# A two-layer decoder trunk on one core: a new order around the six layer norms, and the output with one buffer per tile

## The chip, the cores and the metric

The kernel runs on one core of a Trainium2 chip. Its time is the device time of one execution in microseconds (us). TensorE (PE) multiplies matrices, VectorE (DVE), ScalarE (ACT) and GpSimd (POOL) work on elements, and SyncE (SP) only issues transfers here. Each engine runs its own list of instructions in order and waits on semaphores that other engines raise.

## The reference, cut to what matters

512 prompt tokens and 8 new tokens, 1024 channels, all in float32, go through two layers. Each layer has three blocks, and each block ends in a layer norm of the residual:

```
for l in range(DEPTH):                       # DEPTH = 2
    y = LN(ALPHA * y + 0.5 * swiglu(y, ffn1_wi[l], ffn1_wo[l]))
    y = LN(ALPHA * y + mixer(y))             # layer 0 sparse attention, layer 1 pooling
    y = LN(ALPHA * y + 0.5 * swiglu(y, ffn2_wi[l], ffn2_wo[l]))
```

The last y is the output of 512 x 1024 and 8 x 1024 numbers. Keys, values and pooling states are outputs too.

## The kernel before, in words

The activations stay on the core, channels on the partitions: `xf` has 8 tiles d = 0..7 of 128 channels by 520 tokens. The tokens are worked in two halves h = 0, 1 of 260 columns, `cols(h)`. A float32 product is made of three passes in a faster format: `xh` and `xl` are the high and low parts of x, `w_hi` and `w_lo` those of the weights (`split_hi` on ACT, line 616, and `split_lo` on DVE, line 1672), and the products are w_hi·xh, w_lo·xh and w_hi·xl. POOL makes `xl` (line 2458). Weights come in chunks of 1 MB through SP's queue into two buffers.

The stages run in the order f0, pr, op, f1, f2, pl, f3: f0 to f3 are the four SwiGLU blocks, pr projects and attends, op is attention's output product, pl the pooling mixer. Six of them (f0, op, f1, f2, pl, f3) end in a layer norm, the **tail**. In it each of the two halves goes through the same steps:

- DVE adds the last products to tiles 6 and 7 (`last_residual`, lines 2278, 2071, 2133),
- ACT squares these two tiles (lines 786 and 797),
- PE sums tiles and squares over the channels with a matrix of 1/1024 (`stats`, line 1120; in pl `tile_stats`, line 1610),
- ACT squares the mean (`moments`, line 632), DVE makes 1/variance (`variance`, lines 1687 to 1691), ACT takes the root (`root`, line 636),
- DVE subtracts the mean from each tile and multiplies it by the root (`normalise`, lines 1698 and 1704), ACT applies gain and offset, once for `xh` (line 643) and once for `xf` (line 645) (`affine`; only `xf` after f2 and f3), POOL makes `xl`.

The products of half 0 of a stage's last group end before those of half 1, so the statistics of half 0 are made while PE still multiplies. The statistics of half 1 are handed to the next stage as a function (`left`, or `middle`), which PE calls in its `first_half`: the first two weight chunks j = 0, 1 of the next stage times half 0 of the new x, line 1071. Then it takes half 1 (line 1050). `first_half` serves pr, f1, f2 and f3, whose x comes from a tail, and f0, whose x comes from the input. `two_chunks` calls it.

`first_hi` on ACT (line 860) makes high parts of the third chunk of the next SwiGLU block; the tails of op, f1 and pl hold it (`follow`). The tail of f2 holds `state_columns` (`between`), ACT's copies of the pooling state.

Before it starts, `first_half` waits until both residuals of both halves are done (`s_free`) and until `w_lo` of its first chunk is there (`s_lo`).

At the end of the kernel PE transposes `xf` to token rows (line 1652), 10 pieces of 512 columns (5 token tiles i by 2 column halves q), ACT copies them out of PSUM (line 1015) into `y_out`, which has two buffers, and ACT issues one transfer per token tile (lines 1021 and 1023). Each transfer waits until the one before it has landed: `if i >= 1: act.wait_ge(s_out, 16 * i)`.

## Time and profile before

| | |
|---|---|
| time, median of 3 runs | 1952.11 us (1952.04 to 1952.92) |
| the profiled execution | 1952.89 us, span of its instructions 1950.6 us |
| PE busy | 1849.0 us (95%) |
| DVE busy | 1250.4 us (64%) |
| ACT busy | 875.7 us (45%) |
| POOL busy | 454.1 us (23%) |
| mean granted TensorE clock | 0.979 of full speed |

The span runs from the first to the last instruction; 2.3 us of the time lie around it. A row of the timeline gives the start in us from the span's start, the duration, engine, line, operation, output<-input and count; brackets hold the idle time of the engine before it and what ended it. Rows of consecutive like instructions are merged.

### The profile page before, as it was taken

To read this page: it belongs to the slowest core of one execution; us is meant where nothing else is said; L and a number is where in the kernel's file an instruction comes from. 1 tells how busy PE (TensorE), PEld (TensorE's weight loads), DVE (VectorE), ACT (ScalarE), POOL (GpSimd) and SP (SyncE) were. 2 spreads that over 40 slices of the span, in tenths; PEclk is the share of its full clock that TensorE was granted. 3 is DMA by queue.
4 is the path that set the end of the run, shared out by engine and by line. 5 is a ranking of instruction groups with operands and counts; after the bars stand their busy time and mean duration, and the time that the engine had idled before them with its cause. 6 is when DMAs were issued, how large, how long until landed. Compare 5 with 4: busy or idle time off the path is not lost.

```text
span 1950.6 us, 36339 instructions
## 1 busy us (share of the span) xinstructions
PE 1849.0 (95%) x14532; PEld 1768.8 (91%) x14532; DVE 1250.4 (64%) x1871; ACT 875.7 (45%) x1377; POOL 454.1 (23%) x339
## 2 busy tenths in 40 slices
PE   7999999999989899999999999999998699999996
PEld 7999999996976578999999999999997599999995
DVE  5888832446967525988852288888325798886223
ACT  4455542343334435655552265555413375556123
POOL 3000081241321446100054130000712430003520
PEclk9999999999989999999999999999999799999998
DMA  5333345271110133233332323333323023333221
GB/s 165 91 108 108 108 145 206 72 184 44 28 42 1 39 114 87 66 108 108 108 103 76 103 66 103 104 99 104 98 94 110 2 66 108 108 108 103 83 76 44
DMA packets 260086, 179.79 MB, mean 92 GB/s; under 512 B 10847, under 2 KB 256999, under 8 KB 259462
## 3 DMA queue, kind: packets, MB, share of 16 engines
q1 hardware_dynamic: 249952, 154.90, 27.3%
q0 software_dynamic: 2288, 13.54, 2.0%
q10 hardware_dynamic: 7742, 9.88, 1.9%
q8 instruction: 77, 1.26, 0.3%
q14 instruction: 27, 0.22, 0.0%
HBM read 169.62 MB, written 8.08 MB: 91 GB/s over the span
## 4 chain that ended last, share of the span: by engine, by line
PE 81%; DVE 9%; ACT 4%; issue 3%; DMA 1%; POOL 0%; SPq 0%; ACTq 0%; DVEq 0%; POOLq 0%
PE ps L1145 36%; PE ps L1050 29%; PE ps L1232 3%; PE ps L1423 2%; PE ps L1071 2%; PE ps L1437 2%; PE ps L1237 1%; PE ps L1120 1%; ACT w_hi L616 1%; PE ps L1325 1%; ACT xh L643 1%; ACT xf L645 1%; PE ps L1216 1%; PE ps L1311 1%; DVE w_lo L2172 1%
## 5 line engine op out<-in xcount | busy, mean ns | idle before, releaser
L1672 DVE TENSOR_TENSOR w_lo<-w_raw,w_hi 128x2048 fp32r<-128x2048 f32 (+1 forms) x70 | 173.1, 2473 | 288.1 <-ACT w_hi L616 288.1
L2335 POOL TENSOR_TENSOR hl<-hid_all,hh 128x520 fp32r<-128x520 f32 x88 | 139.6, 1623 | 838.3 <-ACT hh L910 838.3
L1050 PE MATMUL ps<-hh,w_hi 128*128 128x260 f32 x1408 | 293.5, 283 | 0.0
L1050 PE MATMUL ps<-hh,w_lo 128*128 128x260 f32 x1408 | 292.1, 282 | 0.0
L616 ACT CAST w_hi<-w_raw 128x2048 fp32r<-128x2048 f32 (+1 forms) x70 | 126.3, 1805 | 263.2 <-PE ps L1050 236.3
L1050 PEld LDWEIGHTS ps<-hh,w_lo 128*128 128x128 f32 x1408 | 224.4, 188 | 0.1
L1050 PEld LDWEIGHTS ps<-hh,w_hi 128*128 128x128 f32 x1408 | 224.2, 188 | 0.1
L870 ACT CAST w_hi<-w_sum 128x1024 fp32r<-128x1024 f32 x160 | 168.0, 1050 | 117.4 <-DVE w_sum L2154 104.5
L2172 DVE TENSOR_TENSOR w_lo<-w_sum,w_hi 128x1024 fp32r<-128x1024 f32 x160 | 194.8, 1217 | 4.5 <-ACT w_hi L870 4.5
L1050 PE MATMUL ps<-hl,w_hi 128*128 128x260 f32 x1408 | 178.0, 283 | 0.0
L1050 PEld LDWEIGHTS ps<-hl,w_hi 128*128 128x128 f32 x1408 | 172.8, 188 | 0.0
L1145 PE MATMUL ps<-xh,w_hi 128*128 128x260 f32 x640 | 160.4, 283 | 10.7 <-DVE silu_g L2188 6.6
L1145 PE MATMUL ps<-t_hi,w_hi 128*128 128x260 f32 x640 | 161.5, 284 | 0.6 <-DVE w_lo L2172 0.2
L1145 PE MATMUL ps<-t_hi,w_lo 128*128 128x260 f32 x640 | 160.6, 283 | 0.0
L1145 PE MATMUL ps<-xh,w_lo 128*128 128x260 f32 x640 | 159.4, 283 | 0.0
L1145 PEld LDWEIGHTS ps<-xh,w_hi 128*128 128x128 f32 x640 | 120.7, 189 | 13.2 <-DVE silu_g L2188 8.2
L884 ACT ACTIVATE hid_all<-ps 128x260 f32 (+1 forms) x160 | 60.5, 378 | 155.8 <-PE ps L1145 155.8
L1145 PEld LDWEIGHTS ps<-t_hi,w_hi 128*128 128x128 f32 x640 | 121.1, 189 | 1.8 <-issue 0.9
L1145 PEld LDWEIGHTS ps<-t_hi,w_lo 128*128 128x128 f32 x640 | 120.5, 188 | 0.0
L1145 PEld LDWEIGHTS ps<-xh,w_lo 128*128 128x128 f32 x640 | 120.3, 188 | 0.0
L2188 DVE TENSOR_TENSOR silu_g<-silu_g,ps 128x260 f32<-128x260 f32 x160 | 67.3, 420 | 65.6 <-PE ps L1145 62.5
L1145 PE MATMUL ps<-xl,w_hi 128*128 128x260 f32 x640 | 102.9, 283 | 0.0
(330 smaller groups left out, 4432.9 us busy)
## 6 DMA issues: line engine op xcount, KB each, us to landing
w_raw<-in_ffn_wi_dram SPq DMA_DIRECT2D x176, 512.0 KB
w_raw<-in_ffn_wo_dram SPq DMA_DIRECT2D x32, 1024.0 KB
w_raw<-in_ffn_wo_dram SPq DMA_DIRECT2D x16, 768.0 KB
w_raw<-in_attn_w_in_dram SPq DMA_DIRECT2D x8, 1024.0 KB
keys_scratch<-key_half POOLq DMA_DIRECT2D x2, 2048.0 KB, 9.9
w_raw<-in_attn_w_o_dram SPq DMA_DIRECT2D x4, 1024.0 KB
x_in<-in_x_prompt_dram ACTq DMA_DIRECT2D x4, 512.0 KB, 9.7
out_dram<-y_out ACTq DMA_DIRECT2D x4, 512.0 KB
```

The lines of the kernel that those rows point to most:

```text
L616: nc.scalar.copy(w_hi[:, c % 2, 0:n], w_raw[:, c % 2, 0:n]).then_inc(s_hi, 1)
L870: nc.scalar.copy(blocks(st, j)[1][0][:, x], w_sum[:, c % 2, x]).then_inc(s_sums_hi, 1)
L884: nc.scalar.activation(x[..., cols(h)], bank_of(j, b), ACT.Copy).then_inc(s_copy, 1)
L1050: mm = nc.tensor.matmul(ps[0:mc, bank + 2 * m + h, 0:HT], w[:, k, m, 0:mc], x(k)[:, h * HT:(h + 1) * HT], start=first and k == 0 and w is ...
L1071: nc.tensor.matmul(ps[:, 4 * j + 2 * m, 0:HT], w[j][:, k, m, :], x[:, k, cols(0)], start=start, stop=stop)
L1145: mm = nc.tensor.matmul(bank_of(j, bank[p]), w[:, k * P:(k + 1) * P], x[:, k, :], start=p in (1, 2, 4, 5) and k == 0 and w is wh and x is ...
L1232: nc.tensor.matmul(ps[0:mc, bank + h, 0:HT], w[:, k, m, 0:mc], xh[:, k, cols(h)], start=k == 0 and w is wh, stop=False)
L1423: mm = nc.tensor.matmul(ps[:, 2 + t % 2, r * P:(r + 1) * P], attn(B, r)[:, j * P:(j + 1) * P], diag[:, B % 2, r, :], start=True, stop=True)
L1672: nc.vector.tensor_tensor(w_lo[:, c % 2, 0:n], w_raw[:, c % 2, 0:n], w_hi[:, c % 2, 0:n].bitcast(F32), ALU.subtract).then_inc(s_lo, 1)
L2172: nc.vector.tensor_tensor(lo[:, x], w_sum[:, (st.chunk + j) % 2, x], hi[:, x].bitcast(F32), ALU.subtract).then_inc(s_sums_lo, 1)
L2188: nc.vector.tensor_tensor(x, x, bank_of(j, 0), ALU.add).then_inc(s_gate1 if h else s_gate0, 1)
L2335: nc.gpsimd.tensor_tensor(hl[:, k, :], hid_all[:, k, :], hh[:, k, :].bitcast(F32), ALU.subtract).then_inc(s_hl, 1)
```

## The change

Five things are done.

1. `tail` on ACT: after the statistics of half 0 the root comes first, then `split_hi(nxt)` where there is one, then `affine` for the first three tiles (`AHEAD`; none in f2), then `split_hi(nxt + 1)`, then the squares of half 1. Before, `split_hi(nxt + 1)` stood ahead of all `affine` steps, and two tiles (none in f2) ahead of the squares.
2. After the squares of half 1 come two tiles of `affine` instead of three, then `moments` of half 1, then the other tiles, and only then `first_hi` (before: ahead of `moments`).
3. `tail` on DVE: the first three tiles of half 0 are normalised directly after its variance, ahead of `split_lo(nxt)` and of the residual of half 1. Before, all eight came after that residual.
4. `first_half` on PE: chunk 0 takes three tiles, high and low parts, then the statistics of half 1 are made, then chunk 1 takes the three tiles, then both chunks go on tile by tile. The products are the same.
5. The output: `y_out` has five buffers; the ten pieces have an order and PSUM banks of their own, six are copied by ACT and four by DVE, SP issues the five transfers with no wait between them, and the first two pieces are copied by ACT in the tail of f3, ahead of the root of half 1.

```diff
-        y_out = at("y_out", [P, 2, D], offset=h_off)
+        y_out = at("y_out", [P, NQT + 1, D], offset=h_off)
...
+        Y_ORDER = ((0, 0), (0, 1), (1, 0), (1, 1), (2, 0), (3, 0), (4, 0), (2, 1), (3, 1), (4, 1))
+        Y_BANK = {(0, 0): 0, (0, 1): 1, (1, 0): 2, (1, 1): 3, (2, 0): 4, (3, 0): 6, (4, 0): 0, (2, 1): 1, (3, 1): 5, (4, 1): 7}
+        Y_ACT = ((0, 0), (0, 1), (2, 0), (3, 0), (4, 0), (4, 1))
+        Y_DVE = ((1, 0), (1, 1), (2, 1), (3, 1))
...
+        AHEAD = 3
...
@@ block.sync, at its end
+            for i in range(NQT + 1):
+                for of, s_y in ((Y_ACT, s_y_act), (Y_DVE, s_y_dve)):
+                    last = max((n + 1 for n, (t, _) in enumerate(of) if t == i), default=0)
+                    if last > 0:
+                        sp.wait_ge(s_y, last)
+                if i < NQT:
+                    sp.dma_start(outs[0][0, i * P:(i + 1) * P, :], y_out[:, i, :]).then_inc(s_out, 16)
+                else:
+                    sp.dma_start(outs[1].rearrange("b t d -> (b t) d"), y_out[0:DEC, i, :]).then_inc(s_out, 16)
+            sp.wait_ge(s_out, 16 * (NQT + 1))
@@ block.scalar, tail
                 moments(st, 0)
+                root(st, 0)
                 if nxt is not None and not early:
                     split_hi(nxt)
-                root(st, 0)
+                ahead = AHEAD if between is not state_columns else 0
+                affine(n, st, 0, split, order, 0, ahead)
                 if nxt is not None:
                     split_hi(nxt + 1)
-                ahead = 2 if between is None else 0
-                affine(n, st, 0, split, order, 0, ahead)
                 for d in range(KD - 2, KD):
                     act.wait_ge(s_free, first_free + d + 1)
                     nc.scalar.activation(sq[:, d % 2, cols(1)], xf[:, d, cols(1)], ACT.Square).then_inc(s_sq, 1)
-                affine(n, st, 0, split, order, ahead, ahead + 3)
+                affine(n, st, 0, split, order, ahead, ahead + 2)
+                moments(st, 1)
+                affine(n, st, 0, split, order, ahead + 2, KD)
                 if follow is not None:
                     first_hi(plan[follow], nth[follow], 2)
-                moments(st, 1)
-                affine(n, st, 0, split, order, ahead + 3, KD)
                 if between is not None:
                     between()
                 root(st, 1)
...
+            def output(n):
+                act.wait_ge(s_tr, KD + 1 + Y_ORDER.index(Y_ACT[n]) + 1)
+                dst, src = y_half(*Y_ACT[n])
+                nc.scalar.activation(dst, src, ACT.Copy).then_inc(s_y_act, 1)
+
+            def first_output():
+
+                for n in range(2):
+                    output(n)
...
-                     POOL_ORDER if before_pool else range(KD), state_columns if before_pool else None,
+                     POOL_ORDER if before_pool else range(KD), state_columns if before_pool else first_output if nxt is None else None,
...
-            for i in range(NQT + 1):
-                rows = P if i < NQT else DEC
-                for q in range(2):
-                    act.wait_ge(s_tr, KD + 1 + 2 * i + q + 1)
-                    nc.scalar.activation(y_out[0:rows, i % 2, q * 512:(q + 1) * 512], ps[0:rows, 2 * (i % 2) + q, :],
-                                         ACT.Copy).then_inc(s_ev, 1)
-                act.wait_ge(s_ev, KD + 2 * i + 2)
-                if i >= 1:
-                    act.wait_ge(s_out, 16 * i)
...
+            for n in range(2, len(Y_ACT)):
+                output(n)
@@ block.tensor, first_half
-                for k in range(KD + 2):
-                    if k < KD:
-                        pe.wait_ge(s_xh, first_x(st, 0) + k + 1)
-                        tile(0, wh, xh, k, k == 0, False)
-                        tile(0, wl, xh, k, False, False)
-                        if k == 0:
-                            pe.wait_ge(s_hi, st.chunk + 2)
-                        tile(1, wh, xh, k, k == 0, False)
-                    if k == 2 and middle is not None:
-                        middle()
-                    if k >= 2:
-                        pe.wait_ge(s_x, first_x(st, 0) + k - 1)
-                        tile(0, wh, xl, k - 2, False, k == KD + 1)
-                        tile(1, wh, xl, k - 2, False, False)
+
+                def high(j, k):
+                    pe.wait_ge(s_xh, first_x(st, 0) + k + 1)
+                    tile(j, wh, xh, k, k == 0, False)
+                    if j == 0:
+                        tile(0, wl, xh, k, False, False)
+
+                def low(j, k):
+                    pe.wait_ge(s_x, first_x(st, 0) + k + 1)
+                    tile(j, wh, xl, k, False, j == 0 and k == KD - 1)
+
+                for k in range(AHEAD):
+                    high(0, k)
+                for k in range(AHEAD):
+                    low(0, k)
+                if middle is not None:
+                    middle()
+                pe.wait_ge(s_hi, st.chunk + 2)
+                for k in range(AHEAD):
+                    high(1, k)
+                    low(1, k)
+                for k in range(AHEAD, KD):
+                    for j in range(2):
+                        high(j, k)
+                    if k > AHEAD:
+                        for j in range(2):
+                            low(j, k - 1)
+                for j in range(2):
+                    low(j, KD - 1)
@@ block.tensor, at its end
+            for i, q in Y_ORDER:
+                pe.wait_ge(s_xf, tot["t"] - (KD if i < 2 else KD // 2 if q == 0 else 0))
+                if (i, q) in ((4, 0), (2, 1)):
+                    pe.wait_ge(s_y_act, 2)
+                rows = y_rows(i)
+                for d in range(4):
+                    mm = nc.tensor.transpose(ps[0:rows, Y_BANK[i, q], d * P:(d + 1) * P], xf[:, 4 * q + d, i * P:i * P + rows], ident)
+                mm.then_inc(s_tr, 1)
@@ block.vector, tail
                 variance(st, eps, 0)
+                normalise(st, 0, order, 0, AHEAD)
                 if nxt is not None and not early:
                     split_lo(nxt)
                 last_residual(1)
-                normalise(st, 0, order)
+                normalise(st, 0, order, AHEAD, KD)
...
@@ block.vector, at its end
+            for i, q in Y_DVE:
+                dve.wait_ge(s_tr, KD + 1 + Y_ORDER.index((i, q)) + 1)
+                dst, src = y_half(i, q)
+                nc.vector.tensor_copy(dst, src).then_inc(s_y_dve, 1)
```

## Rows read from the trace of the kernel before

**Rows 1.** The page: the chain that ended last, by engine.

```profile
PE 81%; DVE 9%; ACT 4%; issue 3%; DMA 1%; POOL 0%; SPq 0%; ACTq 0%; DVEq 0%; POOLq 0%
```

**Rows 2.** Waits of PE: line, awaited, us in total, times, longest us.

```profile
PE ps L1071 <- ACT xh L643: 14.0, 4, 6.0
```

**Rows 3.** Timeline of PE in the tail of f0 and after.

```profile
384.03 0.48 PE L1071 MATMUL ps<-xh,w_hi 128*128 128x260 f32 x2 [2.64 <-ACT xh L643]
...
388.00 0.76 PE L1120 MATMUL ps<-sum_z,const 128*128 128x260 f32 x2
...
398.24 2.09 PE L1071 MATMUL ps<-xh,w_lo 128*128 128x260 f32 x16
```

**Rows 4.** Stretches there: us, busy (x count) of PE, PEld, DVE, ACT, POOL, clock, DMA share, GB/s.

```profile
384.00:388.00 4.00, 3.97 (x18) 3.60 (x19) 4.00 (x12) 4.00 (x10) 2.23 (x3) 0.61 0.38 56
```

**Rows 5.** Timeline of ACT in the tail of f0.

```profile
381.48 1.90 ACT L616 CAST w_hi<-w_raw 128x2048 fp32r<-128x2048 f32 x1 [2.12 <-PE ps L1050]
383.28 0.60 ACT L643 ACTIVATE xh<-xf,lnp 128x260 fp32r<-128x260 f32 x1
...
391.00 0.39 ACT L632 ACTIVATE hid<-ps 128x260 f32<-128x260 f32 x1 [2.04 <-PE ps L1120]
...
395.17 0.60 ACT L643 ACTIVATE xh<-xf,lnp 128x260 fp32r<-128x260 f32 x1 [0.54 <-DVE xf L1704]
...
399.64 0.59 ACT L645 ACTIVATE xf<-xf,lnp 128x260 f32<-128x260 f32 x1
```

**Rows 6.** Timeline of DVE in the tail of f0.

```profile
374.67 1.79 DVE L1691 RECIPROCAL ps<-ps 128x260 f32<-128x260 f32 x1
379.11 2.29 DVE L1672 TENSOR_TENSOR w_lo<-w_raw,w_hi 128x2048 fp32r<-128x2048 f32 x1 [2.65 <-ACT w_hi L616]
381.42 0.76 DVE L2278 SCALAR_TENSOR_TENSOR xf<-xf,ps 128x260 f32<-128x260 f32 x2
...
382.77 0.41 DVE L1704 TENSOR_TENSOR xf<-xf,ps 128x260 f32<-128x260 f32 x1
...
387.47 2.48 DVE L1672 TENSOR_TENSOR w_lo<-w_raw,w_hi 128x2048 fp32r<-128x2048 f32 x1
```

**Rows 7.** Timeline of POOL in the tail of f0, beside DVE's 387.47.

```profile
388.05 3.18 POOL L2458 TENSOR_TENSOR xl<-xf,xh 128x260 fp32r<-128x260 f32 x2 [0.25 <-ACT xf L645]
```

**Rows 8.** Stretches: PE with two short gaps after the last products (f3).

```profile
1921.50:1926.00 4.50, 3.02 (x14) 2.12 (x12) 4.30 (x13) 2.44 (x6) 0.00 (x0) 1.00 0.00 0
```

**Rows 9.** Timeline of ACT in the tail of op.

```profile
766.94 1.90 ACT L616 CAST w_hi<-w_raw 128x2048 fp32r<-128x2048 f32 x1 [0.33 <-PE ps L1050]
...
776.58 0.39 ACT L632 ACTIVATE hid<-ps 128x260 f32<-128x260 f32 x1 [0.79 <-PE ps L1120]
```

**Rows 10.** Timeline of ACT in the tail of pl.

```profile
1556.93 1.89 ACT L616 CAST w_hi<-w_raw 128x2048 fp32r<-128x2048 f32 x1
...
1564.30 1.47 ACT L860 CAST even_hi<-w_raw 128x1536 fp32r<-128x1536 f32 x1
...
1568.92 0.37 ACT L636 ACTIVATE ps<-ps 128x260 f32<-128x260 f32 x1
```

**Rows 11.** Timeline of DVE, the first step of f2 that awaits the whole tail of f1.

```profile
1154.31 1.56 DVE L2210 TENSOR_TENSOR t_sum<-xf 128x1040 f32<-128x1040 f32 x1 [1.56 <-ACT xf L645]
```

**Rows 12.** Timeline of ACT, the root of half 1 in the tail of f2.

```profile
1509.10 0.37 ACT L636 ACTIVATE ps<-ps 128x260 f32<-128x260 f32 x1 [1.74 <-DVE ps L1691]
```

**Rows 13.** Timeline of PE at the start, `first_half` of f0.

```profile
22.61 1.23 PE L1071 MATMUL ps<-xh,w_hi 128*128 128x260 f32 x4 [1.04 <-ACT w_hi L616]
```

**Rows 14.** Timeline of the tail of f3 and the output, all engines.

```profile
1928.68 3.67 PE L1652 MATMUL ps<-const,xf 128*128 128x128 f32 x16 [2.40 <-ACT xf L645]
...
1936.51 1.06 ACT L1015 ACTIVATE y_out<-ps 128x512 f32<-128x512 f32 x2
1937.60 0.36 ACTq L1021 DMA_DIRECT2D out_dram<-y_out  x1
...
1948.42 0.30 ACTq L1023 DMA_DIRECT2D out_dram<-y_out  x1
```

More of the change, by code:

```diff
@@ L358, in trunk_kernel @@
         s_out = sem("s_out")
+        s_y_act = sem("s_y_act")
+        s_y_dve = sem("s_y_dve")
         s_rope_in = sem("s_rope_in")
@@ L486, in trunk_kernel, with y_rows, y_half @@
         SQUARES = 10
+        Y_ORDER = ((0, 0), (0, 1), (1, 0), (1, 1), (2, 0), (3, 0), (4, 0), (2, 1), (3, 1), (4, 1))
+        Y_BANK = {(0, 0): 0, (0, 1): 1, (1, 0): 2, (1, 1): 3, (2, 0): 4, (3, 0): 6, (4, 0): 0, (2, 1): 1, (3, 1): 5, (4, 1): 7}
+        Y_ACT = ((0, 0), (0, 1), (2, 0), (3, 0), (4, 0), (4, 1))
+        Y_DVE = ((1, 0), (1, 1), (2, 1), (3, 1))
+        def y_rows(i):
+            return P if i < NQT else DEC
+        def y_half(i, q):
+            return y_out[0:y_rows(i), i, q * 512:(q + 1) * 512], ps[0:y_rows(i), Y_BANK[i, q], :]
+        AHEAD = 3
         SIDES = UNITS_OF + 4
@@ L1009, in _ @@
                     ffn(name, after[name])
-            for i in range(NQT + 1):
-                rows = P if i < NQT else DEC
-                for q in range(2):
-                    act.wait_ge(s_tr, KD + 1 + 2 * i + q + 1)
-                    nc.scalar.activation(y_out[0:rows, i % 2, q * 512:(q + 1) * 512], ps[0:rows, 2 * (i % 2) + q, :],
-                                         ACT.Copy).then_inc(s_ev, 1)
-                act.wait_ge(s_ev, KD + 2 * i + 2)
-                if i >= 1:
-                    act.wait_ge(s_out, 16 * i)
-                if i < NQT:
-                    act.dma_start(outs[0][0, i * P:(i + 1) * P, :], y_out[:, i % 2, :]).then_inc(s_out, 16)
-                else:
-                    act.dma_start(outs[1].rearrange("b t d -> (b t) d"), y_out[0:DEC, i % 2, :]).then_inc(s_out, 16)
-            act.wait_ge(s_out, 16 * (NQT + 1))
+            for n in range(2, len(Y_ACT)):
+                output(n)
             act.wait_ge(s_kvo, 16 * 6)
@@ L1644, in _ @@
             left()
-            for i in range(NQT + 1):
-                pe.wait_ge(s_xf, tot["t"] - (KD if i < 2 else 0))
-                rows = P if i < NQT else DEC
-                for q in range(2):
-                    if i >= 2:
-                        pe.wait_ge(s_ev, KD + 2 * (i - 2) + q + 1)
-                    for d in range(4):
-                        mm = nc.tensor.transpose(ps[0:rows, 2 * (i % 2) + q, d * P:(d + 1) * P],
-                                                 xf[:, 4 * q + d, i * P:i * P + rows], ident)
-                    mm.then_inc(s_tr, 1)
+            for i, q in Y_ORDER:
[6 more added lines that the diff above has]
+                mm.then_inc(s_tr, 1)
         @block.vector
@@ L1691, in variance, with normalise @@
                 nc.vector.reciprocal(v, v).then_inc(s_rv, 1)
-            def normalise(st, h, order):
-                n = []
-                for at_ in range(KD + 1):
-                    if at_ < KD:
+            def normalise(st, h, order, begin, end):
+                n = {}
+                for at_ in range(begin, end + 1):
+                    if at_ < end:
                         x = xf[:, order[at_], cols(h)]
-                        n.append(step(nc.vector.tensor_tensor(x, x, moment(0, h), ALU.subtract)))
-                    if at_ == 1:
+                        n[at_] = step(nc.vector.tensor_tensor(x, x, moment(0, h), ALU.subtract))
+                    if at_ == begin + 1:
                         dve.wait_ge(s_rstd, 2 * st.ln + h + 1)
-                    if at_ >= 1:
+                    if at_ > begin:
                         done(n[at_ - 1])
@@ L1717, in tail @@
                 variance(st, eps, 1)
-                normalise(st, 1, order)
+                normalise(st, 1, order, 0, KD)
             def rope_sin(li, m, bank):
```

## The prediction

> **What bounds the kernel now.** I read the page first. The chain that ended last is four fifths PE [rows 1], so only time in which PE idles or runs slowly before the last tail, and the stretch after PE's last product, can be won. Next the waits of PE: the dearest is `first_half` waiting for the first `xh` of a normalised x, four times, 14.0 us [rows 2]. The timeline around one of them shows the pattern: PE ends f0's products at 381.4, idles 2.64 us, restarts at 384.03 [rows 3], and for the next 4 us its granted clock is 0.61 of full, the level of 1.2 GHz for most of it [rows 4]. The products of `first_half` start 0.12 us apart at full clock (16 in 2.09 with the last one's drain) and 0.22 apart at half. In PE's own terms the tail of f0 holds 96 products (11.5 us) and the statistics of half 1 (2.6 us), 14.1 us, and takes from 381.4 to 400.2, 18.8: 4.6 lost, 2.6 to the idle gap and 2.0 to the clock. Then I laid ACT and DVE beside it [rows 5, 6]: both have nothing to do before the products end and are full after. Last the end of the kernel [rows 14]: the five transfers of the output are issued from 1937.60 to 1948.42, every 2.70 us, one after the landing of the other.
>
> **The change part by part.** Times are of the profiled execution; steps are start to start. One subtract or multiply of DVE is 0.336 us (14 of them from 382.77 to 387.47), so a tile is 0.67 [rows 6]. One `affine` instruction is 0.50 (9 steps from 395.17 to 399.64), so a tile with `xh` and `xf` is 0.99 [rows 5].
>
> *Tail of f0 into pr.* DVE's 1/variance ends at 376.46; three tiles (2.0 us) and the root (0.37) then fit before `split_lo` at 379.11, in an idle stretch of 2.65 [rows 6]. ACT splits the next chunk until 379.0 as before, and applies three tiles until 381.96 (2.97), while PE still multiplies. The second split can only start when the last product frees its buffer, at 381.48 [rows 5], so it comes 0.5 late. POOL's first `xl` now fall on `split_lo`. Beside one, POOL needed 3.18 for two and DVE 2.48 instead of 2.29 [rows 6, 7]: I add 0.2 to the residual (bounds 0 and 0.2). PE waits for that residual, 381.6 + 0.7, and starts at 382.5 instead of 384.03. The gap is 1.1 us. In the tail of f3 PE has gaps of 0.61 and 0.87 in 4.5 us and the clock stays 1.00 [rows 8], so I take full clock here. 18 products of chunk 0 (2.2), statistics done 2.96 after their start (the distance from 388.00 to the mean's square at 391.00 [rows 3, 5]) at 387.65, `first_half` ends at 382.5 + 14.1 = 396.6 instead of 400.2: 3.5 won. Does x come in time? On ACT: split, squares and two tiles until 386.4, mean's square at 387.65, three tiles until 390.9, root, first tile of half 1 at 391.8, instead of 395.17 [rows 5]. Its eighth `xh` is there at 399.4; PE needs it at 396.6 + 7 x 0.48 = 400.0. It holds by 0.6. **3.5**, bounds 2.5 and 3.7.
>
> *Tail of f1 into f2.* The same, but `first_hi` (1.37 a step) now stands between the last tile of half 0 and the root, and delays it: half 1 starts on ACT 2.0 us earlier, not 3.4. Its eighth `xh` is now late for PE by about a microsecond, and DVE's `t_sum`, which follows ACT's last `xf` at once [rows 11] and heads an unbroken chain of DVE to PE's fifth product of the stage, moves by the same 2.0. **2.0**, bounds 1.2 and 2.8.
>
> *Tail of op into f1.* Its products of half 1 are short, so 1/variance ends at 766.2, 0.7 before they end. The three tiles (2.0) now push the residual from 766.89 to 768.2, so PE starts only 0.4 earlier (769.05 for 769.49), and ACT starts its first tile at 767.3 where it started the split at 766.94 [rows 9]. From there ACT is full: the list split, tiles, squares, mean, `first_hi`, root took 11.99 us in pl with no gap (1556.93 to 1568.92) [rows 10], and the new order has the same entries. So 0.36 is lost at the front and the 0.79 before the mean's square [rows 9] is won, if the statistics are in time. 0.4, less a bit for the clock, which with a gap of 2.2 us may fall here. **0.3**, bounds -0.5 and 0.9.
>
> *Tail of pl into f3.* Here ACT had no gap at all [rows 10]. It now waits for the first normalised tile (1557.6 instead of 1556.93) and the root of half 1 comes 0.65 later. PE's gap of 6 us stays, because the residual of half 1 is now behind three tiles. **-0.6**, bounds -1.2 and 0.
>
> *Tail of f2 into pl.* DVE bounds this stage. Three tiles leave its list, 2.0, and the root finds ACT idle 1.74 before [rows 12]. **1.7**, bounds 1.2 and 2.0.
>
> *Start of f0.* PE waits 1.04 for the second split [rows 13]; 18 products of chunk 0 now fill it, at 0.22 each. Four or five of them, worth 0.12 later. **0.6**, bounds 0 and 1.04.
>
> *Tail of f3 and output.* The last product ends at 1921.65. DVE normalises five tiles instead of eight after the residual, 1922.4 to 1925.8 (was 1927.7), 1/variance is ready at 1928.4 (was 1930.4). But ACT now awaits two transposed pieces. PE gets half 0 at 1927.1; four transposes take 0.92 (16 in 3.67 at half clock) and a copy 0.53 [rows 14], so the second copy ends and the root starts at 1929.5, 1.1 after it could. `xf` is complete at 1935.6, 1.0 earlier. Then the last three pieces are transposed until 1938.0 (0.92, 0.92, 0.5). ACT has four copies from 1935.6, the last at 1938.1; DVE four of about 0.6 (its copies are not in this stretch; I take ACT's price), the last at 1937.7. So SP issues tile 0 at about 1930, tile 1 at 1936.2, 2 at 1937.4, 3 at 1938.4, the short one at 1938.8. The last issue before was at 1948.42 and the span ended 2.2 later. With 2.2 to 2.7 to land, and 0.3 for transfers in each other's way, the span ends at 1941.3 instead of 1950.6. **9.3**, bounds 8 and 10.5 (the clock of the last transposes is worth 1).
>
> The Trainium skill (DMA: Bandwidth & Descriptors, Anatomy of one DMA) puts a transfer at about 2.0 us fixed and the bytes at 436 GB/s, as an estimate 3.2 us for 512 KB; the trace shows an issue every 2.70. By the page the end would be some 0.5 later.
>
> Sum: 3.5 + 2.0 + 0.3 - 0.6 + 1.7 + 0.6 + 9.3 = 16.8. The profiled execution took 1952.89 (span 1950.6 and 2.3 around it), so 1936.1; the median of the runs lies 0.8 below it, so **1935.3 us**.
>
> **The rivals.**
>
> *A, the clock falls all the same* in the tails of f0 and f1. For it: it stood at 1.00 until after PE had restarted at 384.03, so it does not answer to the gap at once [rows 3, 4]. Against: the gap is 1.1, not 2.64, and [rows 8]. 3.1 us at half (4.00 at 0.61 [rows 4]) would cost 1.6 in each: gain 13.6, 1938.5. Beside it, the Trainium skill (TensorE: Matmul & The Clock Gate, A second HAM failure mode) says that frequent short idle spells can make the clock swing between its levels; the stretch with two such spells does not show it.
>
> *B, the transfers do not overlap*: each of the last three takes its 2.7 behind the other. From 1936.2 that is 1944.3, and 2.2 for the short one: 1946.5, 5.2 less, 1940.5. For it: all are on the same 16 engines. Against: most of the 2.7 need not be data; nothing shown here tells.
>
> *C, the tails give nothing*: ACT's list is as long as before, and in op and pl it sets the pace. If it does in f0 and f1 too, only the output gains: 1942.8. Against: ACT idles 2.12 before the split at 381.48 and 2.04 before the mean's square [rows 5].
>
> *D, slower*: PE's new order begins every `first_half` with a burst and then waits for the residual, POOL or the statistics, and the clock stays at half through it. Each product at half costs 0.10 to 0.12 more; `first_half` has 96, five times. From 172 products more at half (21 us) the kernel is slower by over 0.2%; all of four tails would cost 46 less 17, 1981. Against: the rows show full clock again from about 388.2 under steady products [rows 4].
>
> **How the numbers follow.** Forecast 0.66, A 0.13, B 0.10, C 0.08, D 0.03. The time is that of the forecast. Its bounds, all at the good end, give 1931.2; all at the bad end 1941. The range of 1931.0 to 1940.5 holds the forecast nearly whole, A and half of B. About 0.2% (3.9 us) is what a measurement of this kernel can tell from no change. Forecast, A, B and C are faster by more: 0.95 with a little off for several shortfalls together; same 0.02, slower 0.03.
>
> **What would show it.** In the changed profile: the wait of `first_half` for `xh` is down from 14.0 to about 6 (pl alone), with PE's gap after f0 and f1 near 1.1 and the clock 1.00 in the 4 us behind it; on ACT in f1 `first_hi` directly ahead of the root; the residual in op and pl behind three tiles; the root in f3 about 1 us after DVE's reciprocal, behind two copies; five issues on SP, the last some 17 us after PE's last product of f3 (it was 26.8). The prediction is wrong if the clock is at half in f0 and f1, if the last landing comes more than 21 us after PE's last product, or if a wait for POOL's `xl` appears in `first_half`.

## The result and the profile after

The changed kernel takes 1936.07 us (median of 4 runs, 1933.81 to 1936.65) beside 1952.07 (1949.44 to 1952.92) of the kernel before on the same chip: ratio 0.9913, 95% interval 0.9901 to 0.9925. That is 16.0 us less. The forecast was 1935.3, the range 1931.0 to 1940.5. The profiled execution took 1936.2, its span 1933.9.

To say where the time came from, I cut both spans at instructions that both kernels have: DVE's last residuals, DVE's `t_sum`, PE's w_lo·xh products of chunk 1 of `first_half` (merged as x16). The columns are differences of start times in the two profiles; the last row runs from the step of DVE that f3's last product releases to the end of the span. "None" marks a stretch for which the prediction had no term.

| stretch | before | after | gain | predicted |
|---|---|---|---|---|
| span start to f0's first product with `t_hi` | 49.86 | 48.83 | 1.0 | 0.6 |
| f0's residual of half 1 to the x16 products of pr | 16.82 | 13.17 | 3.65 | 3.5 |
| from there through attention to op's residual of half 0 | 359.40 | 359.78 | -0.4 | none |
| from there to the `t_sum` of f1 | 31.20 | 30.54 | 0.66 | 0.3 |
| f1's residual of half 0 to the `t_sum` of f2 | 34.34 | 32.16 | 2.18 | 2.0 |
| f2's residual of half 1 to pl's residual of half 0 | 48.73 | 46.74 | 2.0 | 1.7 |
| pl's 1/variance of half 0 to the `t_sum` of f3 | 23.09 | 24.57 | -1.5 | -0.6 |
| f3's last product to the end | 28.9 | 19.9 | 9.0 | 9.3 |

They sum to 16.7, the difference of the spans; predicted were 16.8. (The products between these stretches take the same time to 0.05 us.)

Timeline of PE in the changed kernel, in the tail of f0, where [rows 3] are those of before:

```profile
381.26 0.47 PE L1093 MATMUL ps<-xh,w_hi 128*128 128x260 f32 x2 [0.90 <-DVE w_lo L1707]
...
383.49 0.60 PE L1157 MATMUL ps<-sum_z,const 128*128 128x260 f32 x2
...
393.57 2.09 PE L1093 MATMUL ps<-xh,w_lo 128*128 128x260 f32 x16
```

PE idles 0.90 us instead of 2.64. Stretches of 4 us that begin at the restarts in f0 and op and around the one in f1 (columns as in [rows 4], which showed 0.61):

```profile
381.20:385.20 4.00, 3.94 (x26) 3.77 (x27) 4.00 (x11) 4.00 (x7) 1.86 (x3) 1.00 0.78 139
764.60:768.60 4.00, 3.84 (x25) 3.48 (x26) 4.00 (x11) 4.00 (x7) 1.76 (x3) 1.00 0.00 0
1128.00:1132.00 4.00, 3.48 (x24) 3.37 (x25) 4.00 (x13) 4.00 (x7) 1.85 (x4) 1.00 0.80 231
```

The clock is at its upper level in all three. ACT in the same tail [rows 5] has no idle time before the split, and 0.87 instead of 2.04 before the mean's square:

```profile
380.94 1.90 ACT L640 CAST w_hi<-w_raw 128x2048 fp32r<-128x2048 f32 x1
...
386.32 0.39 ACT L656 ACTIVATE hid<-ps 128x260 f32<-128x260 f32 x1 [0.87 <-PE ps L1157]
...
390.50 0.61 ACT L667 ACTIVATE xh<-xf,lnp 128x260 fp32r<-128x260 f32 x1 [0.55 <-DVE xf L1739]
```

The waits of PE in `first_half` (columns as in [rows 2], where ACT's `xh` stood with 14.0): what is left is one gap in pl, one in op and two short ones in f0 and f1.

```profile
PE ps L1093 <- DVE xf L2169: 6.1, 1, 6.1
PE ps L1093 <- DVE xf L2107: 2.1, 1, 2.1
PE ps L1093 <- DVE w_lo L1707: 1.8, 2, 0.9
```

Timeline of ACT in the tail of pl: the mean's square of half 1 before, with no idle time ahead of it (the rest in [rows 10]), and then the changed kernel:

```profile
1565.67 0.38 ACT L632 ACTIVATE hid<-ps 128x260 f32<-128x260 f32 x1
```

```profile
1548.46 0.60 ACT L667 ACTIVATE xh<-xf,lnp 128x260 fp32r<-128x260 f32 x1 [0.61 <-DVE xf L1739]
...
1556.64 0.39 ACT L656 ACTIVATE hid<-ps 128x260 f32<-128x260 f32 x1 [0.69 <-PE ps L1647]
...
1559.90 1.47 ACT L894 CAST even_hi<-w_raw 128x1536 fp32r<-128x1536 f32 x1
1561.27 0.38 ACT L660 ACTIVATE ps<-ps 128x260 f32<-128x260 f32 x1
```

This list had no gap before. Now it has two, 0.61 and 0.69, and `first_hi` (1.37 a step) stands directly ahead of root. One more thing differs there. PE restarts 4.6 and 4.7 us behind the start of 1/variance of half 0 in the two kernels, after a gap of 6.0 to 6.1 us and at half clock, but in the changed kernel the clock comes back later. The stretch of 3 us that begins 7.6 us behind 1/variance, before and after:

```profile
1562.40:1565.40 3.00, 3.00 (x20) 2.77 (x19) 2.99 (x2) 3.00 (x6) 2.65 (x2) 0.98 0.00 0
```

```profile
1553.30:1556.30 3.00, 3.00 (x15) 2.73 (x14) 2.48 (x2) 2.65 (x7) 1.26 (x1) 0.71 0.00 0
```

The statistics of half 1 end 10.95 us behind 1/variance instead of 10.17.

The end of the kernel, timeline of PE, DVE and ACT and then SP's issues ([rows 14] before):

```profile
1921.10 0.38 ACT L660 ACTIVATE ps<-ps 128x260 f32<-128x260 f32 x1
1924.65 5.38 PE L1688 MATMUL ps<-const,xf 128*128 128x128 f32 x24 [2.37 <-ACT xf L669]
1929.21 0.69 DVE L2347 COPY y_out<-ps 128x512 f32<-128x512 f32 x1 [0.16 <-PE ps L1688]
1930.07 0.59 ACT L874 ACTIVATE y_out<-ps 8x512 f32<-8x512 f32 x1 [1.54 <-PE ps L1688]
1921.23 0.37 SPq L628 DMA_DIRECT2D out_dram<-y_out  x1
1927.53 0.37 SPq L628 DMA_DIRECT2D out_dram<-y_out  x1
...
1930.68 0.31 SPq L630 DMA_DIRECT2D out_dram<-y_out  x1
```

The last product releases DVE at 1913.99; the last issue comes 16.7 behind that and the end 19.9 (before 26.8 and 28.9).

### The profile page after: what moved, and what is told of

The parts are those of the page before. It is cut to its first block, busy times and chain, and to the rows that moved or that the text cites. A ratio compares the mean times of both kernels' runs of the same rounds, so it can differ in the third digit from the quotient of the medians.

```text
span 1933.9 us, 36347 instructions
## 1 busy us (share of the span) xinstructions
PE 1849.3 (96%) x14532; PEld 1768.4 (91%) x14532; DVE 1251.2 (65%) x1875; ACT 874.0 (45%) x1373; POOL 453.0 (23%) x339
## 4 chain that ended last, share of the span: by engine, by line
PE 82%; DVE 8%; ACT 5%; issue 3%; DMA 1%; POOL 0%; ACTq 0%; DVEq 0%; POOLq 0%
PE ps L1182 36%; PE ps L1072 29%; PE ps L1269 3%; PE ps L1460 2%; PE ps L1474 2%; PE ps L1093 2%; PE ps L1274 1%; PE ps L1157 1%; PE ps L1362 1%; ACT xf L669 1%; ACT xh L667 1%; ACT w_hi L640 1%; PE ps L1253 1%; PE ps L1348 1%; DVE w_lo L2208 1%
```

## The experiments

Each run was timed against the kernel before on its own chip; a ratio stands with its interval. An execution's start and its attention part differ from run to run by up to 2.6 us each (below), so verdicts rest on the stretches of the table above, which in the runs that leave them alone repeat to 0.05 us for f0, op and f1, to 0.2 for f2, to 0.4 for the last one and to 0.8 for pl. The last two differ with the moment at which the clock comes back in them. In pl that moment is 8.9 to 9.4 us behind 1/variance where the stretch takes 24.35 to 24.58 (five executions), and 10.4 and 10.5 where it takes 25.06 and 25.14. In the last stretch it is 13.6 us behind the last product, amid the last transposes, where the stretch takes 19.6, and 16.5, behind all of them, where it takes 19.9. Pl and the last stretch are therefore to be compared between executions with like clocks.

**1. Output alone.** The changed kernel with ACT's and DVE's tail and `first_half` as before.

```diff
-                normalise(st, 0, order, 0, AHEAD)
...
-                for k in range(AHEAD):
-                    high(0, k)
...
+                for k in range(KD + 2):
```

> The new output alone (five buffers, SP's transfers, the order of the pieces, the first two copies in the tail of f3); tails and first_half as before. Terms add: in the tail of f3 the two copies delay the root of half 1 by 0.5, PE transposes the last 24 tiles in 5.4 us from the fourth xf tile of half 1 on, and the span ends 3.9 after it, near 1943.9, 6.7 shorter than 1950.6, with everything before f3's last product where it was (1921.7). Rival (the output gains only together with the shorter tail of f3): under 4 us. Ratio to the kernel before 0.9966 by the first, above 0.998 by the second.

1946.35 us (1945.61 to 1948.21), ratio 0.9967 (0.9955 to 0.998). From the last product to the end 22.2 instead of 28.9: 6.8. The tails are as before: 17.14, 31.30, 34.40, 48.75 and 23.09 in the order of the table, with the 2.64 gap behind f0.

**2. Tails alone.** The kernel before with the new tails and the new `first_half`, and its own output.

```diff
+        AHEAD = 3
...
-                for k in range(KD + 2):
+                for k in range(AHEAD):
+                    high(0, k)
```

> The new tails and first_half alone, output as before with two buffers and a transfer awaiting the one before. Terms add: f3's last product 7.7 us earlier as in the changed kernel, in f3 the normalisation of three tiles ahead gives 2.0 more, the transfers are then issued 2.70 apart as before: span 9.7 shorter, near 1940.9, ratio 0.995. Rival (the tails' gain is given back later, in attention or by slower transfers): less than 7.

1942.86 us (1941.54 to 1943.33), ratio 0.9948 (0.9932 to 0.9965). The stretches are those of the changed kernel (13.17, 30.53, 32.16, 46.72, 24.58), and the last one is 26.9, 2.0 less than before: DVE's part of the new tail gives that in f3. 6.8 and 2.0 are 8.8 of the 9.0, so the two halves add up and neither needs the other. No run tells PE's new order (part 4 of the change) from the new lists of ACT and DVE (parts 1 to 3).

**3. One transfer behind the other.** Tests rival B.

```diff
+                if i > 0:
+                    sp.wait_ge(s_out, 16 * i)
                 if i < NQT:
                     sp.dma_start(outs[0][0, i * P:(i + 1) * P, :], y_out[:, i, :]).then_inc(s_out, 16)
```

> The changed kernel, but each of SP's five transfers awaits the landing of the one before; five buffers, copies and transposes unchanged. If the overlap of the transfers carries the output's gain: tile 1 is issued at the same place (13.6 us after f3's last product), tiles 2 and 3 and the short one 2.7 apart behind it, and the end is 3.9 later than in the changed kernel (span 1937.8). Rival (the last three transfers are bound by the bytes that the queue moves, so waiting costs little): under 1 us later.

From the last product to the end 23.8 instead of 19.9, and SP's issues again every 2.70 us: the overlap is worth 3.8 (4.2 beside the executions with 19.6). The time is 1938.63 us (1937.08 to 1940.35), ratio 0.9931 (0.9915 to 0.9948). The profiled span, 1934.8, is only 0.9 longer than the changed kernel's, because its start was 0.9 and its attention part 2.6 shorter. The windows of the changed kernel between 1930 and 1932 show what overlapped transfers share: 406 GB/s, so 1.29 us for 512 KB. The rest of the 2.70 is no data: in the kernel before, where transfers also went one by one, 1.2 us of each step move nothing.

```profile
1939.80:1941.00 1.20, 1.08 (x6) 0.68 (x4) 0.00 (x0) 0.28 (x1) 0.00 (x0) 0.50 0.00 0
```

**4. PE held.** Tests what gap and clock are worth by giving both back: PE starts `first_half` of pr and f2 only at the fourth `xh`.

```diff
+                if st in (plan["pr"], plan["f2"]):
+                    pe.wait_ge(s_xh, first_x(st, 0) + AHEAD + 1)
```

> The changed kernel, but in pr and f2 PE's first_half waits for the fourth xh tile of half 0 before it starts, which puts back a gap of about 3.6 us after the products of f0 and f1 (0.9 in the changed kernel). If a gap of this length costs the clock too, as in the kernel before: granted clock 0.5 for about 3 us behind the restart and 3.6 to 4.3 us lost in each of the two, 7 to 8 in all. Rival (the clock does not fall, the half clock of the kernel before had another cause): 2.7 us each, 5.4 in all, clock 1.00.

1945.11 us (1943.5 to 1947.97), ratio 0.9962 (0.9948 to 0.9976). The stretch of f0 takes 18.95 instead of 13.17, that of f1 36.72 instead of 32.16: 5.8 and 4.6, of which the longer gap (3.85 instead of 0.90) is 2.95 each. The rest, 2.8 and 1.6, fits the clock: in f0 it was at half until 6.1 us behind the restart, in f1 from 1.4 to 4.8 behind it. The end moved by 8.9, with the start and attention 1.4 shorter in this run. Timeline and stretch behind the restart in f0:

```profile
383.67 0.77 PE L1093 MATMUL ps<-xh,w_hi 128*128 128x260 f32 x2 [3.85 <-ACT xh L667]
```

```profile
384.00:388.00 4.00, 4.00 (x19) 4.00 (x19) 2.16 (x1) 0.90 (x2) 3.46 (x2) 0.50 0.13 19
```

19 products in 4 us where the changed kernel does 27. The rival, a gap at full clock, falls.

**5. Residual first** in op and pl (the two tails for which `early` is true), on DVE and, with the second split, on ACT. DVE's part:

```diff
                 variance(st, eps, 0)
+                if early:
+                    last_residual(1)
                 normalise(st, 0, order, 0, AHEAD)
```

> The changed kernel with one part set back in op and pl alone: VectorE adds the residual of half 1 ahead of the three normalised tiles instead of behind them, and ScalarE writes the xh of the next stage's second tile ahead of the normalised tiles instead of behind. Theory (the loss of 1.5 us in pl comes from starting the tiles before the residual, since ScalarE's tiles then wait for root and xh): from the residual to pl's last sum of half 1 0.8 to 1.5 us less than the 20.9 us of the changed kernel, and op 0 to 0.7 us more than its 20.1; in all about 0.8 us earlier than the changed kernel. Rival (the loss in pl comes from the place of first_hi behind the moments, which this run keeps): pl's stretch stays within 0.2 us, and the end with it.

1937.47 us (1936.55 to 1939.15), ratio 0.9922 (0.9909 to 0.9936). Both expectations miss. Pl takes 25.18; the clock came back late in it (10.5), and with that the unchanged pl takes 25.06 and 25.14. Op takes 32.64 instead of 30.54: 2.1 worse, more than before the change. PE's timeline and the stretch behind it in op:

```profile
763.36 0.48 PE L1095 MATMUL ps<-xh,w_hi 128*128 128x260 f32 x2 [2.64 <-ACT xh L667]
```

```profile
763.30:767.30 4.00, 3.75 (x17) 3.33 (x18) 4.00 (x12) 4.00 (x10) 2.23 (x3) 0.65 0.00 0
```

The gap is 2.64 again and the clock falls. PE also waits 0.18 for its second `xh`, and the statistics end 2.3 us later than in the changed kernel, where the gap was 2.12 and the clock stayed at 1.00. ACT has nothing ahead of them to do and waits 2.28.

**6. `first_hi` ahead of `moments`** in op, f1 and pl, as it was.

```diff
+                if follow is not None:
+                    first_hi(plan[follow], nth[follow], 2)
                 moments(st, 1)
                 affine(n, st, 0, split, order, ahead + 2, KD)
-                if follow is not None:
-                    first_hi(plan[follow], nth[follow], 2)
```

> The changed kernel with one part set back: the next half's first xh (first_hi) is issued on ScalarE ahead of the moments' sums and normalised tiles of half 1 instead of behind them, in op, f1 and pl. Theory: ScalarE stood idle 0.87 us in f1 and 0.69 us in pl ahead of the moments, and first_hi of 1.3 us stood straight ahead of root in f1 and pl, with 1.23 us of idle time on VectorE behind it; set back it fills the idle time, so f1's stretch from residual to last sum is 0.9 us shorter than 19.5, pl's 0.7 shorter than 20.9, op's the same: 1.6 us in all. Rival: the moments and the root are then late by the whole of first_hi less the idle time, 0.4 to 0.6 us later, and nothing or a small loss comes of it.

1934.21 us (1933.57 to 1935.17), ratio 0.9905 (0.989 to 0.9921). Pl takes 23.81. The clock came back at 9.1 in it, for which the unchanged pl takes 24.35 to 24.57, so the edit is worth 0.5 to 0.8, where the theory said 0.7. Op takes 30.58, the same, but not for the same reason. Its gap is 2.12 as in the changed kernel, and this time the clock falls behind it:

```profile
763.42 0.48 PE L1093 MATMUL ps<-xh,w_hi 128*128 128x260 f32 x2 [2.12 <-DVE xf L2107]
```

```profile
763.40:767.40 4.00, 3.98 (x21) 3.81 (x22) 4.00 (x11) 4.00 (x7) 1.69 (x3) 0.69 0.00 0
```

The statistics end 1.3 us later than in the changed kernel, and nothing is lost, since `first_hi` (1.37) now runs on ACT while they are made. So 1.3 of the 2.3 by which the statistics were late in run 5 is the price of the clock alone, and it reaches the end of the tail only as far as ACT has no work left to put ahead of `moments`.

F1 takes 32.03 instead of 32.16, where 0.9 less was expected. ACT in f1:

```profile
1132.21 1.48 ACT L894 CAST even_hi<-w_raw 128x1536 fp32r<-128x1536 f32 x1 [0.68 <-DMA w_raw<-in_ffn_wi_dram]
1133.59 0.38 ACT L656 ACTIVATE hid<-ps 128x260 f32<-128x260 f32 x1
```

The weights are not there yet. `first_hi` waits 0.68 for them and delays the mean's square by 1.2 (from 18.59 to 19.78 behind f1's residual of half 0), which takes back most of what the root gains: it comes 0.2 earlier. In f1 the load decides, not ACT.

**7. PE kept busy ahead of the last transposes**, with spare products into a bank that nobody reads at that time. They have 260 columns each, not the 128 of the expectation.

```diff
+                if (i, q) in ((0, 0), (2, 0)):
+                    busy(14 if i == 0 else 26)
                 pe.wait_ge(s_xf, tot["t"] - (KD if i < 2 else KD // 2 if q == 0 else 0))
```

> The changed kernel with 14 and 26 spare products of 128 columns on TensorE ahead of the first output tile's 4 transposes and ahead of the last 24, written to a bank that nobody reads. Theory: the transposes ran at a granted clock of 0.50 because TensorE stood idle ahead of them; with the spare products the clock is up when they start, one takes 0.11 to 0.12 us instead of 0.224, the last output copies come 1.5 to 2 us earlier, and the end 0.5 to 1.0 us earlier, since the last three transfers of 1.29 us each then bound it. Rival: the clock stays at 0.50 over the transposes for all the products, and the end is the same or later by up to 1 us.

1935.38 us (1932.06 to 1935.72), ratio 0.9911 (0.9896 to 0.9926). The clock is 1.00, and the transposes come 0.11 us apart instead of 0.21:

```profile
1920.79 1.53 PE L1694 MATMUL ps<-const,xf 128*128 128x128 f32 x12
1923.29 1.53 PE L1694 MATMUL ps<-const,xf 128*128 128x128 f32 x12 [0.97 <-ACT xf L669]
```

The last copy ends 1.4 us earlier (15.3 behind the last product instead of 16.7). The end follows by 0.3: 19.6, where the unchanged version of this stretch took 19.9 in the two executions whose transposes all ran at half clock. In three others it took 19.6 as well: there the clock came back by itself 13.6 us behind the last product, and the last copy ended at 15.5. DMA shows why more speed than that buys nothing, in stretches of 1 us:

```profile
1924.00:1925.00 1.00, 0.82 (x8) 0.46 (x6) 1.00 (x2) 0.81 (x3) 0.00 (x0) 1.00 0.48 197
1925.00:1926.00 1.00, 0.00 (x0) 0.00 (x0) 0.27 (x1) 0.44 (x1) 0.00 (x0) 1.00 1.03 414
...
1927.00:1928.00 1.00, 0.00 (x0) 0.00 (x0) 0.00 (x0) 0.00 (x0) 0.00 (x0) 1.00 0.99 401
1928.00:1929.00 1.00, 0.00 (x0) 0.00 (x0) 0.00 (x0) 0.00 (x0) 0.00 (x0) 1.00 0.67 193
```

From the second transfer on (issued at 1923.67) the engines carry the last 1.6 MB without a break. The end comes 6.1 us behind that issue, here and in runs 5, 6, 8, 9, 11 and 12, whose transposes sped up too, and 6.4 in the changed kernel's first execution and in runs 4 and 10, where they stayed at half clock and the copies were slowest.

**8. All together**: 5, 6 and 7, and in f3 root of half 1 ahead of the two output copies.

```diff
+                if between is first_output:
+                    root(st, 1)
                 if between is not None:
                     between()
-                root(st, 1)
+                if between is not first_output:
+                    root(st, 1)
```

> The three edits together (residual of half 1 ahead of the tiles in op and pl, first_hi ahead of the moments, spare products ahead of the last transposes), and in f3 root of half 1 ahead of the two first output copies instead of behind them. Theory: 0.8 + 1.6 + 0.7 us, and 0 to 1 from the root (it waited 0.4 us or less behind the copies after the variance): 3 to 4 us less than the changed kernel, a span near 1930.5. Rival: the edits to the queue of ScalarE only move its waits, and the end stays within 1 us of the changed kernel's.

1933.76 us (1932.89 to 1934.86), ratio 0.99 (0.9885 to 0.9916). Pl takes 23.28, the last stretch 19.4, but op 31.77, 1.2 more than the changed kernel, with the gap of 2.64 and a falling clock as in 5 (there 2.1 more, since `first_hi` stood late). In pl the residual first pays only together with `first_hi` early: beside executions with like clocks 5 alone gave nothing, 6 alone 0.5 to 0.8, both 1.3. With both, ACT's list runs as in [rows 10] with 0.1 before the mean's square.

**9. The version that these point to**: op as in the changed kernel, pl as in 8, `first_hi` early, f3 as in 8.

```diff
+                swap = st is plan["pl"]
+                if swap:
+                    last_residual(1)
                 normalise(st, 0, order, 0, AHEAD)
```

> The version that the earlier runs point to: the changed kernel's order in op; in pl the residual of half 1 and ScalarE's second split ahead of the three tiles; first_hi ahead of the moments; in f3 root of half 1 ahead of the two output copies, with the spare products. Theory, from the stretches of the combined run: pl 1.3 us shorter, f1 0.1, op 0, the stretch from f3's last product to the end 0.5: 1.9 us less than the changed kernel beside it. Rival: the stretches add up but the end moves by less than 1 us, since the start and the attention take 1 to 3 us more or less from one build to the next.

1931.92 us (1930.55 to 1932.67), ratio 0.9891 (0.9875 to 0.9908). Op 30.59, f1 32.12, pl 23.35, last stretch 19.4.

**10. Root ahead of the copies alone** (the diff of 8, nothing else).

> The changed kernel with root of half 1 of the last norm ahead of the two first output copies on ScalarE, and nothing else. Theory (the root stood about 0.4 us behind the copies after VectorE had the variance): from f3's last product to the end 0.3 us less than 19.9; the rest of the combined run's 0.5 came from the spare products. Rival: the first transfer is then late by the root's wait and the end is the same.

1935.53 us (1933.68 to 1936.22), ratio 0.991 (0.9893 to 0.9926). Last stretch 19.7. The transposes of this execution ran at half clock to their end, as in the two that took 19.9, so the root ahead gives 0.2, near the 0.3 of the theory. With the spare products as well, in 8 and 9, it gives the same: 19.4 for 19.6.

**11. The changed kernel again**, on the chip of 9 and 10.

> The changed kernel itself, once more. Both theories: a ratio of 0.991 to 0.992 as before; the stretches within tails the same to 0.1 us, and the start up to f0's residual of half 1 and the attention different by up to 3 us, as in the other runs. If the start comes out the same to 0.3 us, the differences seen there belong to the builds.

1935.5 us (1933.8 to 1935.76), ratio 0.9905 (0.9889 to 0.9922). The stretches of f0, op, f1 and f2 repeat to 0.02 us, pl takes 25.06 (24.57), the last one 19.6 (19.9), attention 358.93 (359.78). Pl's 0.5 is the clock: it comes back 1.0 us later, and ACT waits so much longer for the statistics, 1.20 for 0.69:

```profile
1556.42 0.39 ACT L656 ACTIVATE hid<-ps 128x260 f32<-128x260 f32 x1 [1.20 <-PE ps L1647]
```

**12. The version of 9 again.**

> The best version once more. Open is whether its early start (f0's first w_hi product of the third chunk at 46.6 instead of 48.8 to 49.1 in the changed kernel, because the products behind 20.5 ran at 0.12 instead of 0.22 us from the first on) belongs to the build or falls by chance. If by chance: that product comes anywhere from 46.5 to 49.1, the stretches within the tails repeat to 0.1 us except pl's (0.7), and the median lies between 1931.5 and 1934. If it belongs to the build: 46.6 again to 0.2 us.

1933.1 us (1932.22 to 1935.13), ratio 0.9906 (0.9889 to 0.9922). Op 30.58, f1 32.15, pl 23.17, last stretch 19.4, and `t_hi` at 47.84 instead of 46.55: the early start of 9 belongs to the execution, not to the build. Over the stretches the version is 1.2 to 1.3 us better in pl (beside executions with like clocks) and 0.2 to 0.5 in the last stretch. Whole runs do not settle it. On the chip that ran both, its four times (1930.55 to 1932.67) lie below the four of the changed kernel (1933.8 to 1935.76), but the ratios are 0.9891 and 0.9906, those of the changed kernel 0.9913 and 0.9905, and their intervals overlap.

## Why the prediction was right

The sum of the terms was right to 0.1 us, each term to 0.4, with one exception of 0.9. The closeness of the sum is luck in part: five terms were 1.4 too small together, and two terms and the unforeseen 0.4 of attention 1.6 too large. The median was missed by 0.8, because I took 0.8 off for the difference between profiled execution and median; in the changed kernel it was 0.1.

*Tail of f0, 3.5 predicted, 3.65.* Each step is in the trace: gap 0.90 for 1.1, clock 1.00 behind it, and first tile of half 1 on ACT 10.10 us behind the residual of half 1 (13.75 before). What I added for POOL's `xl` beside `split_lo` was not due: that split took 2.29, as alone. Run 4 supports that the term is gap plus clock. A, which let the clock fall all the same, is refuted by the stretches after. The Trainium skill (TensorE: Matmul & The Clock Gate, A second HAM failure mode) warns that frequent short idle spells can make the clock swing; the waits of 0.90 in f0 and of 0.90, 0.25 and 0.24 in f1 did not do so here.

*F1, 2.0 predicted, 2.18; f2, 1.7 and 2.0.* `first_hi` stands directly ahead of the root as forecast, with 1.23 of idle time behind it on DVE. That this cost could be avoided by its old place was my theory after the result; run 6 refuted it for f1.

*Op, 0.3 predicted, 0.66.* I took 0.4 and cut it for a clock that might fall behind a gap of 2.2. It was 2.12 and the clock held, as in eight of the nine other runs with that gap; in run 6 it fell, so that it held is in part luck. I had sized the order by what ACT's list saves. Run 5 shows a second gain: with the residual first the same tail has the gap of 2.64, a falling clock and late statistics, and takes 2.1 more, for which ACT's empty wait is needed too (run 8: 1.2 more).

*Pl, -0.6 predicted, -1.5, outside its bounds of -1.2 and 0: the step that failed.* It said that ACT waits for the first normalised tile, 0.65 later. That is there: ACT starts its list 0.7 later. It took ACT's list to run without a gap from there, with no term for the statistics, and the root comes 1.5 later. Ahead of the mean's square stands an idle time of 0.69, where [rows 10] have none. Two things make it. `first_hi`, moved behind the tiles, no longer covers the wait: the list is through at 10.3 us behind 1/variance. And the statistics end at 10.95 instead of 10.17, as the clock comes back at 9.4 instead of 7.7; with statistics at 10.2 there would be no wait. I had counted the same entries in the list and not asked which of them filled a wait, nor when PE would be done. With `first_hi` early alone (run 6) the loss is 0.7, about what I had forecast; the order of 8 brings the stretch back to 23.2 to 23.4 in three runs, 23.09 before. The size is in part chance: the same pl took 24.35 to 25.14 in six other runs, so the loss is 1.3 to 2.0, by the moment at which the clock comes back. That moment was 7.7 in both executions of the old tail and 8.9 to 10.5 in the twelve of the new ones; why it is later is not shown.

*Start of f0, 0.6 predicted, 1.0.* The wait of 1.04 is gone. Part of the 1.0 is PE's pace, which rose at 26.5 before and at 25.8 after (below). The execution with the new `first_half` that is nearest to 26.5 is that of run 8, with 26.2: its start is 0.8 shorter than before, so the change is worth 0.6 to 0.8.

*Tail of f3 and output, 9.3 predicted, 9.0.* Last issue 16.7 behind the last product, 17 predicted. On the way errors cancel. The root stood 0.4 behind DVE's reciprocal, not 1.1, and x was complete 0.8 earlier than forecast. Against that, from the complete x to the end of the last transpose there are 2.9 us, not 2.4, since the four small ones take as long as the others; and the last issue is followed by 3.2 us, not 2.5. B is refuted by run 3: the overlap is worth 3.8 to 4.2 of the 5.2 that I had priced. The Trainium skill (DMA: Bandwidth & Descriptors, Anatomy of one DMA) gives 436 GB/s for the bytes of a transfer that GpSimd issues; SP and ACT issue these, and the trace has 401 to 414. Its end, 0.5 later than mine, would be 20.2 behind the last product; the runs had 19.6 to 19.9.

*C* (the tails give nothing) is refuted by run 2, where they alone give 10.4 us between the medians. *D* did not come: with PE's new order the clock stays at 1.00 in f0 and f1 in every run but 4, and in op in all whose gap is 2.12 but run 6. Run 4 shows how near the other side lies: a start 2.95 later costs 5.8, and the stretch is then 2.1 longer than before the change.

*Not predicted*: the 0.4 that attention took back. The same kernel differs there by 0.85 between two executions, and the runs by 2.6 (357.17 to 359.78), so nothing has to be explained by the change. The time goes with how long PE's clock is at half in that stretch, by the traces' clock records: 17.1 us in run 3 (357.17), 20.5 in eight executions with the new `first_half` (358.20 to 358.93), 23.9 in the changed kernel's first and in runs 1, 2 and 6 (359.13 to 359.78). The kernel before had 20.5 and 359.40, so the 3.4 us more at half clock can account for the 0.4. No run holds the clock fixed there, so this is a likeness and not a proof.

## What to carry to other kernels

Cut two profiles at instructions that both have, and compare stretches: here three of them repeat to 0.05 us where whole runs differ by 2, and a wrong term shows at once. Where a stretch does not repeat, look first for the moment at which the clock changes in it. When an instruction is moved in an engine's list, ask what wait it filled in its old place, not only what it delays in the new one. And before feeding the last transfers faster, look for the first of the unbroken chain of transfers: only its issue moves the end.

## What the hardware showed

*The clock behind a gap of PE.* Gaps of 0.90 us left the granted clock at 1.00 in the next 4 us in f0 and f1 in every run that has them. A gap of 2.12 in op left it there in nine executions and came with 0.69 in a tenth, that of run 6, with the same instructions ahead of it. Gaps of 2.64 came with 0.58 to 0.69 in seven places of three kernels and with 0.80 in run 8, 3.85 with 0.50 and 0.68, and 6.1 (pl) with 0.50 and 0.61. So here 2.12 can go either way. What a fall costs depends on what waits: 1.3 us of later statistics in op cost nothing in run 6.

*A start by chance.* In the first microseconds the products come 0.22 us apart until some moment and 0.12 behind it. The moment is 18.6 in two executions (7 and 9), 23.4 to 24.5 in six and 25.7 to 28.2 in six, with the same instructions up to there in twelve of the fourteen. It moves the rest of the kernel by up to 2.5 us: f0's first `t_hi` product comes at 46.55 and 49.09 in two builds whose start is the same. The column of the granted clock does not show it. The stretch from 21 to 25 us of the changed kernel, and of run 7:

```profile
21.00:25.00 4.00, 4.00 (x21) 4.00 (x20) 3.13 (x3) 3.97 (x4) 4.00 (x3) 1.00 0.63 164
```

```profile
21.00:25.00 4.00, 4.00 (x34) 3.93 (x34) 3.17 (x2) 3.97 (x4) 4.00 (x3) 1.00 0.64 174
```

Both say 1.00, with 21 and 34 products in 4 us. The clock records of each trace begin only at that moment (25.8 and 18.6 in these two), and time without a record reads 1.00: at the start of the span the pace of the products has to be read, not the clock. This spread is large enough for the 2 to 3 us between the executions of one kernel, though only profiled ones can be read.

*Transposes at half clock* come 0.21 us apart, those that give 8 rows no closer than those that give 128, and at full clock 0.11. Halving them brought the last copy 1.4 us forward and the end 0.3; beyond that the transfers were the chain.
